# Two-block diffusion transformer on one core: the second block's mixer with hi and lo parts, two heads side by side, and both mLSTM directions in one tile

## The reference, cut to what matters

```python
def hybrid_mixer(h, w_in, gate_bias, g_q, g_k, g_mh, w_out):
    proj = (h @ w_in).astype(jnp.float32)
    mq, mk, mv, mo, mg, aq, ak, av = jnp.split(proj, idx, axis=-1)
    gates = mg.reshape(B, S, 4, M_HEADS).transpose(2, 0, 3, 1) + gate_bias[:, None, :, None]
    hm = bidirectional_mlstm(heads(mq, 4), heads(mk, 4) * (64 ** -0.5), heads(mv, 4),
                             gates[0], jax.nn.log_sigmoid(gates[1]), gates[2], jax.nn.log_sigmoid(gates[3]))
    hm = rms_norm(hm, g_mh) * jax.nn.sigmoid(mo)
    qa = partial_rope(rms_norm(heads(aq, 8), g_q), pos) * (64 ** -0.5)
    ka = partial_rope(rms_norm(heads(ak, 8), g_k), pos)
    ha = dilated_attention(qa, ka, heads(av, 8))
    return jnp.concatenate([hm, ha], axis=-1) @ w_out
```

## Time and profile before

| | us |
|---|---|
| median of 3 runs (lowest, highest) | 3451.45 (3450.44, 3454.13) |
| the profiled execution, its own time | 3450.88 |
| its span | 3449.1 |
| PE busy | 3188.1 (92%) |
| DVE busy | 1912.9 (55%) |
| ACT busy | 1013.9 (29%) |

### The profile page before, as it was taken

One profiled execution on the slowest core, in us unless ns is written; L12 is line 12 of the kernel. 1 busy time (PEld: TensorE's weight loads), 2 busy tenths in 40 slices (PEclk: granted clock), 3 DMA queues, 4 the chain that ended last, 5 costly groups with the idle time before them and its releaser, 6 DMA issues.

```text
span 3449.1 us, 36019 instructions
## 1 busy us (share of the span) xinstructions
PE 3188.1 (92%) x14535; PEld 2523.5 (73%) x14546; DVE 1912.9 (55%) x2700; ACT 1013.9 (29%) x1458; POOL 28.4 (1%) x31
## 2 busy tenths in 40 slices
PE   4999999898889999899969999799999989699998
PEld 3788888776677888788847888578877745377886
DVE  6876554645555554666565544566655534454444
ACT  2322122335442222322223222322223334232222
POOL 2000000000000000000000000000000000000000
PEclk6999999998999999999989999899999959699999
DMA  4443332110034433355512433145532200023221
GB/s 187 128 141 122 110 129 85 53 55 10 1 115 136 153 129 110 110 188 187 170 66 98 161 133 122 61 161 188 190 133 78 76 8 1 12 86 104 91 94 54
DMA packets 101889, 365.26 MB, mean 106 GB/s; under 512 B 11235, under 2 KB 12515, under 8 KB 101469
## 3 DMA queue, kind: packets, MB, share of 16 engines
q1 hardware_dynamic: 97644, 351.65, 30.7%
q10 hardware_dynamic: 2944, 6.29, 0.5%
q0 software_dynamic: 1136, 5.03, 0.4%
HBM read 360.83 MB, written 2.10 MB: 105 GB/s over the span
## 4 chain that ended last, share of the span: by engine, by line
PE 86%; DVE 9%; ACT 3%; issue 1%; DMA 1%; another core or an unknown queue 0%; ACTq 0%; POOL 0%; DVEq 0%; SPq 0%
PE ps L191 23%; PE ps L192 23%; PE ps L193 23%; PE ps L195 4%; PE ps L196 2%; DVE WL L183 1%; PE ps L2470 1%; DMA STG<-in_w_modt 1%; PE ps L2534 1%; DVE DUMP L304 1%; PE ps L2266 1%; PE ps L2269 1%; PE ps L507 1%; ACT WH L178 1%; DVE RAW L1301 1%
## 5 line engine op out<-in xcount | busy, mean ns | idle before, releaser
L191 PE MATMUL ps<-HH,WH 128*128 128x512 f32 x2464 | 980.3, 398 | 35.1 <-DVE HL L564 28.4
L192 PE MATMUL ps<-HL,WH 128*128 128x512 f32 x2464 | 968.9, 393 | 0.0
L193 PE MATMUL ps<-HH,WL 128*128 128x512 f32 x2464 | 968.6, 393 | 0.0
L178 ACT ACTIVATE WH<-RAW 128x1024 fp32r<-128x1024 f32 x456 | 456.7, 1047 | 569.0 <-PE ps L193 410.1
L183 DVE TENSOR_TENSOR WL<-RAW,WH 128x1024 fp32r<-128x1024 f32 x456 | 538.5, 1221 | 100.8 <-ACT WH L178 100.7
L191 PEld LDWEIGHTS ps<-HH,WH 128*128 128x128 f32 x2464 | 468.3, 190 | 144.3 <-issue 44.2
L192 PEld LDWEIGHTS ps<-HL,WH 128*128 128x128 f32 x2464 | 468.5, 190 | 100.3 <-issue 4.1
L193 PEld LDWEIGHTS ps<-HH,WL 128*128 128x128 f32 x2464 | 467.6, 190 | 100.9
L815 DVE SCALAR_TENSOR_TENSOR XT<-ps,DER,XT 128x512 f32<-128x512 f32 x512 | 342.9, 682 | 272.2 <-PE ps L193 257.7
L191 PE MATMUL ps<-GH,WH 128*128 128x512 f32 x1056 | 414.0, 392 | 19.1 <-DVE XT L815 14.3
L192 PE MATMUL ps<-GL,WH 128*128 128x512 f32 x1056 | 412.0, 390 | 0.0
(11 more groups left out here) (330 smaller groups left out, 2482.1 us busy)
## 6 DMA issues: line engine op xcount, KB each, us to landing
RAW<-in_w_modt SPq DMA_DIRECT2D x200, 512.0 KB, 4.6
RAW<-in_ffn_wi SPq DMA_DIRECT2D x176, 512.0 KB, 4.5
RAW<-in_ffn_wo SPq DMA_DIRECT2D x88, 512.0 KB, 4.7
RAW<-in_w_gu SPq DMA_DIRECT2D x88, 512.0 KB, 4.3
RAW<-in_w_in SPq DMA_DIRECT2D x44, 512.0 KB, 3.6
RAW<-in_w_down SPq DMA_DIRECT2D x44, 512.0 KB, 4.3
RAW<-in_w_out SPq DMA_DIRECT2D x16, 512.0 KB, 3.7
MU<-in_w_mod SPq DMA_DIRECT2D x8, 384.0 KB, 9.4
```

Of the source, the lines that this page charges most:

```text
L178: act.e.activation(u.hi, u.ld.view, ACT.Copy).then_inc(u.hi_done.sem, 1)
L191: pe.e.matmul(out, wh, x[0], start=first, stop=False)
L192: pe.e.matmul(out, wh, x[1], start=False, stop=False)
L193: m = pe.e.matmul(out, wl, x[0], start=False, stop=last)
```

## The change

- **Gates beside the projection.** `GT` becomes `G` with 36 partitions: the forward direction on partitions 0 to 3, the backward on 32 to 35. `MlGates`, `MlScan` and `MlTurnU` handle both directions together, and they are put into the list through `lag`, behind the first chunks of the projection. The log, the exponential and the scans stand in the mixer's first steps no more.
- **Hi and lo parts.** Queries and keys of both generators, the running maximum, the inverse denominators and the norm's factor are split by `HiLo` (hi on ACT, lo on DVE), and the matmuls on them become three (or two, where the other side is exact) in fp32r. The parts lie over `RAW` slots 2 to 5 and over the tensors that they replace.
- **Two heads side by side.** `DilScore`, `DilPV` and the new `DilQuot` issue the heads of a pair one behind the other, on array rows 0 to 63 and 64 to 127 (scores) or on array columns 0 to 63 and 64 to 127 (values). The values become the stationary operand, the output comes out already with features on partitions, and the division by the denominator is a product with a matrix that is spread by a matmul (`DilDen`, `DilQuot`) in place of a product and a transpose.
- **Sums of both directions together** (`MlSum`): two `A x V`, then two `A x 1`, the latter on 4 columns at array columns 0 and 32.
- **Order.** `dilated` goes first in `side_by_side`, has three pieces for each of 16 pairs, and every fourth round gives `mlstm` another piece. The split of the mLSTM half of `MIX` and of the first `w_out` tile is at the end of `mlstm`; the other half is split after the last `DilQuot`. The weight slots are 0 and 1 until the last score is done.

The core of the diff:

```diff
+class MlGates(Step):
+    def scalar(self, act):
+        m, t = self.m, self.t
+        act.wait_ge(*self.ready)
+        act.e.activation(m.EM, m.MG, ACT.Abs).then_inc(t[0].sem, 1)
+        act.wait_ge(*t[0])
+        act.e.activation(m.EM, m.EM, ACT.Exp, scale=-1.0).then_inc(t[1].sem, 1)
+        act.wait_ge(*t[1])
+        act.e.activation(m.EM, m.EM, ACT.Ln, bias=1.0).then_inc(t[2].sem, 1)
+class MlScan(Step):
+    def vector(self, dve):
+        m, t, rows = self.m, self.t, self.rows
+        dve.wait_ge(*m.gates)
+        dve.e.scalar_tensor_tensor(m.MG, m.MG, 0.0, m.EM, ALU.min, ALU.subtract).then_inc(t[0].sem, 1)
+        dve.wait_ge(*t[0])
+        dve.wait_ge(*m.ones)
+        for d in range(2):
+            dve.e.tensor_tensor_scan(rows(m.B, d), m.ONES[32 * d:32 * d + 4, :], rows(m.MG, d), 0.0,
+                                     ALU.mult, ALU.add).then_inc(t[1 + d].sem, 1)
+        dve.wait_ge(*t[2])
+        dve.e.tensor_tensor(m.U, m.U, m.B, ALU.subtract).then_inc(t[3].sem, 1)
+        dve.wait_ge(*t[3])
+        for d in range(2):
+            u = rows(m.U, d)
+            dve.e.tensor_tensor_scan(rows(m.MG, d), u, u, -BIG, ALU.max, ALU.max).then_inc(t[4 + d].sem, 1)
+        dve.wait_ge(*t[5])
+        dve.e.tensor_tensor(m.EM, m.B, m.MG, ALU.add).then_inc(t[6].sem, 1)
+    def scalar(self, act):
+        m = self.m
+        act.wait_ge(*self.t[6])
+        act.e.activation(m.EM, m.EM, ACT.Exp, scale=-1.0).then_inc(self.em.sem, 1)
...
 class MlBroadcast(Step):
-        pe.wait_ge(*m.scan[1].t[3])
-        pe.wait_ge(*m.landed)
+        pe.wait_ge(*m.sel)
+        pe.wait_ge(*self.split.done)
         for d in range(2):
+            r = slice(32 * d, 32 * d + 4)
             pe.wait_ge(*self.free[d])
-            pe.e.matmul(m.P.banks[1 + d], m.SEL[:, h, :], m.MG[:, d, :], start=True, stop=True).then_inc(self.spread[d].sem, 1)
+            pe.e.matmul(m.P.banks[1 + d], m.SEL[r, h, :], m.MGH[r, :], start=True, stop=False)
+            pe.e.matmul(m.P.banks[1 + d], m.SEL[r, h, :], m.MGL[r, :], start=False, stop=True).then_inc(self.spread[d].sem, 1)
...
-        p, par = h // 2, h % 2
-        r = slice(64 * par, 64 * par + 64)
+        p, r = h // 2, slice(64 * (h % 2), 64 * (h % 2) + 64)
+        js = slice(self.j * 128, self.j * 128 + 128)
+        pe.wait_ge(*m.qsplit.done)
+        pe.wait_ge(*m.ksplit.done)
         for t in self.qkfree:
             pe.wait_ge(*t)
-        pe.e.matmul(m.P.banks[0], m.K[r, p, self.j * 128:self.j * 128 + 128], m.Q[r, p, :],
-                    start=True, stop=True).then_inc(self.qk.sem, 1)
+        pe.e.matmul(m.P.banks[0], m.KH[r, p, js], m.QH[r, p, :], start=True, stop=False)
+        pe.e.matmul(m.P.banks[0], m.KH[r, p, js], m.QL[r, p, :], start=False, stop=False)
+        pe.e.matmul(m.P.banks[0], m.KL[r, p, js], m.QH[r, p, :], start=False, stop=True).then_inc(self.qk.sem, 1)
...
+class MlSum(Step):
+    def tensor(self, pe):
+        m, h, j = self.m, self.x.h, self.x.j
+        pe.wait_ge(*m.landed)
+        for d in range(2):
+            full = self.x.prod.full(d)
+            pe.wait_ge(*self.x.prod.done[d])
+            if j == 0:
+                pe.wait_ge(*self.free[d])
+            x = pe.e.matmul(m.P.banks[1 + d][:, full], m.V[:, j, h * 128:(h + 1) * 128], m.A[:, self.x.slot[d], full],
+                            start=j == 0, stop=True, skip_group_check=j > 0)
+        x.then_inc(self.summed.sem, 1)
+        for d in range(2):
+            full = self.x.prod.full(d)
+            x = pe.e.matmul(m.P.banks[3][32 * d:32 * d + 4, full], m.OH[:, 3 - h:7 - h], m.A[:, self.x.slot[d], full],
+                            start=h + j == 0, stop=True, skip_group_check=True)
+        x.then_inc(self.done.sem, 1)
...
 class DilScore(Step):
-        pe.e.matmul(b, w.Q[r, j, n * 128:(n + 1) * 128], w.K[r, j, :], start=True, stop=True)
...
+        def product(Q, K, first):
+            for par in range(2):
+                r = slice(64 * par, 64 * par + 64)
+                m = pe.e.matmul(w.P.banks[4 + par], Q[r, j, n * 128:(n + 1) * 128], K[r, j, :], start=first, stop=True,
+                                skip_group_check=not first)
+            return m
+
+        product(w.QH, w.KH, True)
         pe.wait_ge(*w.table)
+        for par in range(2):
+            pe.e.matmul(w.P.banks[4 + par], w.CB[:, 0:128], w.CB[:, 128 + o:128 + o + 512], start=False, stop=True,
+                        skip_group_check=True)
+        product(w.QH, w.KL, False)
+        product(w.QL, w.KH, False).then_inc(self.scored.sem, 1)
...
 class DilPV(Step):
-            m = pe.e.matmul(P.banks[7][:, hs * 64:hs * 64 + 64], w.PT[:, self.v % 3, i * 128:(i + 1) * 128],
-                            w.V[:, i, hs * 64:hs * 64 + 64], start=i == 0, stop=i == 3)
+            for par in range(2):
+                hs = 2 * j + par
+                m = pe.e.matmul(P.banks[7][64 * par:64 * par + 64, j * 128:(j + 1) * 128], w.V[:, i, hs * 64:hs * 64 + 64],
+                                w.PT[:, self.q % 2, par, i * 128:(i + 1) * 128], start=i == 0, stop=i == 3, skip_group_check=True)
...
+class DilDen(Step):
...
+            dve.e.tensor_tensor(w.D[:, 2 * par:2 * par + 2, :].rearrange("p r (h t) -> p r h t", t=128),
+                                w.P.ID.rearrange("p (a b t) -> p a b t", a=1, b=1).broadcast_to([128, 2, 2, 128]),
+                                w.DEN[:, s, par:8:2].rearrange("p (r h o) -> p r h o", h=2, o=1).broadcast_to([128, 2, 2, 128]),
+                                ALU.mult).then_inc(self.diag[par].sem, 1)
...
+class DilQuot(Step):
...
+            m = pe.e.matmul(P.banks[6][64 * par:64 * par + 64, :], P.ONE[:, 0:64], w.D[:, 2 * par:2 * par + 2, :],
+                            start=True, stop=True, skip_group_check=True)
...
+        x = w.MIX[:, 4:8, n * 128:(n + 1) * 128]
+        dve.wait_ge(*self.copied)
+        dve.wait_ge(*self.spread)
+        dve.e.tensor_tensor(x, x, w.P.banks[6].rearrange("p (c t) -> p c t", t=128), ALU.mult).then_inc(self.done.sem, 1)
...
+                def gates(ready):
+                    yield
+                    self.add(MlGates(m, ready))
+                    yield
+                    self.add(MlScan(m))
+                    yield
+                    yield
+                    self.add(MlTurnU(m, pr))
...
-            with ExitStack() as both:
-                self.add(Begin([self.group, self.roped, self.turned, self.evacd]))
-                m = Mlstm(self, both, MQt, MKt, MVt, MOt, GT, MIX)
-                w = Dilated(self, both, DQt, DKt, DVt, MIX)
-                self.side_by_side(self.mlstm(m), self.dilated(w, CF, cf), extra=5)
-                ready = [w.out[3].done, m.last]
-            return self.out_projection(mi, a["w_out_2"], MIX, ready, following)
-    def mlstm(self, m):
+            lent = [t for s in range(2, NRAW) for t in self.inslot[s].users]
+            self.add(Begin([self.group, self.roped, self.turned, self.evacd] + lent))
+            self.slots = [0, 1]
+            rounded = lambda n, shape, address: self.at(n, shape, F32R, address)
+            at = lambda n: self.address[n] if n in self.address else self.address[self.name(n)]
+            QH, KH = (rounded(n, [128, 4, T], at("RAW") + (2 + 2 * i) * 4096) for i, n in enumerate(("QH", "KH")))
+            QL, KL = rounded("QL", [128, 4, T], at("MIX") + 8192), rounded("KL", [128, 4, T], at("DKt"))
+            w = Dilated(self, outer, QH, QL, KH, KL, DVt, MIX, self.XT[:, 0:4, T:W])
+            m.tiles(outer, sb("MQH", [128, 2, T], F32R), rounded("MQL", [128, 2, T], at("MQt")),
+                    sb("MKH", [128, 2, T], F32R), rounded("MKL", [128, 2, T], at("MKt")))
+            mix = Mix(MIX, rounded("MH", [128, 8, T], at("MQt")), rounded("ML", [128, 8, T], at("MIX")))
+            self.side_by_side(self.dilated(w, CF, cf, DQt, DKt), self.mlstm(m, mix, a["w_out_2"]), extra=4)
+            self.slots = list(range(NRAW))
+            for s in range(2, NRAW):
+                self.inslot[s] = Lent([w.score[15].scored])
+            self.add(Begin([w.quot[3].done]))
+            self.add(MixSplit(self, mix, range(4, 8), [w.quot[3].done]))
+            self.out_products(mi, a["w_out_2"], mix, {}, following)
+        return [self.over]
+    def mlstm(self, m, mix, w_out):
         self.add(MlTables(m))
-        self.add(MlGates(m))
+        m.mgsplit = self.add(HiLo(self, m.MG, m.MGH[:, :], m.MGL[:, :], []))
+        m.qsplit = self.add(HiLo(self, m.Q[:, :, :], m.QH[:, :, :], m.QL[:, :, :], []))
...
+        for j in range(4):
+            w.qsplit[j] = self.add(HiLo(self, DQt[:, j, :], w.QH[:, j, :], w.QL[:, j, :], []))
+            w.ksplit[j] = self.add(HiLo(self, DKt[:, j, :], w.KH[:, j, :], w.KL[:, j, :], []))
+        last = len(w.pairs)
+        for q in range(last + 2):
+            if 1 <= q <= last:
+                self.add(DilCount(w, q - 1))
+            if q < last:
+                self.add(DilScore(w, q))
+                yield
```

(11 more changed lines are left out.)

483 lines of the change are left out of this document (237 added, 246 removed).

## The result

| | before | after |
|---|---|---|
| median of 4 runs, us (lowest, highest) | 3451.52 (3450.44, 3454.13) | 3399.76 (3399.12, 3401.05) |
| ratio, 95% interval | | 0.9849 (0.9832 to 0.9866) |
| span of the profiled execution, us | 3449.1 | 3397.7 |
| PE busy, us | 3188.1 | 3129.7 |

The account below looks back on a forecast made before the run. PE's work was taken to bound the projection and the mixer's first two stretches, a PE, DVE and ACT chain the tail. 3450.9 less 70 in the mixer plus 16 in the projection gave 3397 us, range 3368 to 3424.

Parts of the forecast that it names:

- The gates in the projection: Projection: gate work ahead of a weight split on ACT and a reciprocal on DVE delays PE, costing 16 us.
- The 2.5 us more for the clock: Projection: PE's pause lets its clock fall for a while, adding about 2.5 us to the 13.4 us delay.
- some 13 us: Projection: a PE gap of this length near 2622, given as a sign that would show the prediction right.
- The price of a pair: Dilated attention, two heads at full clock: scores 1.55, values and transposes 1.61, second head's transposes 0.43; 3.6 us.
- The price of a unit: mLSTM unit at full clock: score 0.8 and sums 2.3, so 3.1 us where it was 3.7.
- Phase 2: Mixer proper, fourth pair's score to last mLSTM sum: nine pairs, sixteen units, quotients, waits and clock; 92 us (80 to 105).
- the 5 us for a clock that rises late: Middle of the mixer proper: the clock rises about 10 us into this stretch, which costs 5 us.
- The rival with ACT and DVE in turn: Mixer's middle: ACT and DVE work in series, 112 us where 92 was forecast, total 3417; chance 0.14.
- Phase 1: Mixer proper, start to fourth pair's score, still at 1.2 GHz: 27 us (22 to 40), 5 of it waiting.
- Phase 3: Mixer's tail after the last mLSTM sum, with four dilated pairs in it: 63 us (50 to 72).
- the last two pairs, some 9.5 each on their chain: End of the tail: maximum, exponential, count, transposes and values of two dilated pairs, 19 us together.
- The output projection: After the mixer: it starts on the mLSTM half of MIX and a split weight tile, so nothing is added.

Follow-up runs that it names:

- the gap filled: Changed kernel plus six f32 matmuls on PE between the projection and the first dilated score, where PE stood still 5.2 us; 3399.42 us.
- the run with six pairs: Changed kernel with extra=2 for extra=4 until the last mLSTM sum, none after, so six dilated pairs stand in the tail, not four; 3411.79 us.
- the run with two: Kernel with gates in pieces and f32 scores (3385.99 us), with extra=0: two dilated pairs' scores stand behind the last mLSTM sum; 3379.97 us.

## Why the prediction was right, step by step

- **The gates in the projection** (forecast 16, measured 14.4). Each step came where it was put: `WH` 2617.39 for 2617.7, the end of `WL` 2619.7 for 2620.0, the reciprocal 2629.40 for 2629.6, the rotation 2633.60 for 2633.8, PE's next chunk 2636.18 for 2636.4. The 2.5 us more for the clock were 1.2 (14.4 less the 13.2 at 2636.18); behind the pause the first products do start further apart (2636.18, 2636.75, 2637.18, 2637.60, then 0.23 apart). The chain was followed instruction by instruction through the new order with durations from the trace, and so came out to 0.3 us. Only the sign was misnamed: the gap of "some 13 us" on PE is one of 7.42, since the 13.2 is how late PE is, 4.0 of it from the stall before.
- **The price of a pair** (forecast 1.55 for the scores, measured 1.54). The sum is right and its terms are not: the parts were put at 1.32 and take 1.00, the mask at 0.24 and takes 0.54. The 1.32 from the first block's window attention already had a small mask and its changes of mode in it (a product with `CB` of 128 columns at 838.88, which the rows leave out). So this is partly luck. That the heads overlap, as the rows had it, is shown by the run that puts them one behind the other.
- **The price of a unit** (forecast 3.1). The score is 0.78, the sums, 2.75 before, are 1.9 to 2.2 by the lengths of the two directions: 2.9 on average. I had taken half a us off the sums, and they lost 0.5 to 0.8.
- **Phase 2** (forecast 92, measured 82.1). Three terms were too large: the 5 us for a clock that rises late (it rose at 2805, with the phase), the waits (PE was idle 2.9 us for 4), and the units (16 x 0.2 = 3). The rival with ACT and DVE in turn is out: they are busy 42.4 and 42.6 us beneath PE's 79.2. The Trainium skill, "TensorEngine Tiling (Array Packing)", section "PSUM Bottleneck", has the reading of PSUM as a possible limit after a fourfold speedup by packing; with the twofold packing here it is not seen to act.
- **Phase 1** (forecast 27, measured 33.3). I summed PE's work at half clock. It is busy 22.0 us there, as summed; but I gave the waits 5 where they were 11.3, at the start for the splits of queries and keys, and then for the table load, the maximum and the exponential. With the gap filled the clock was 1.00 for about the first 9 us of the phase and nothing was won, so there the clock isn't the cause.
- **Phase 3** (forecast 63, measured 73.5). The mLSTM's part was right: 8.1 us to the first product (forecast 8.5), 25.0 for the heads (26), 10.0 for the norm (9.3). What failed is the end: "the last two pairs, some 9.5 each on their chain", 19. From the first `L2453` at 2930.64 to 2960.96 it is 30.3 us: 7.9 to the fifteenth pair's scores at 2938.49, for what stands in the queues ahead of them (half of the thirteenth pair's transposes, the twelfth's values, a quotient), then 9.7 and 12.8. The forecast had no term for the 7.9, and the last two pairs took 22.5 for 19. Pairs were taken as covered by the mLSTM's chain, on whose queues they stand in turn with it; the run with six pairs shows 8 us for each one more, the run with two shows 7.0 for each one less. The 73.5 also lies above the 72 that was given as this phase's bound.
- **The output projection** (forecast 0, measured 2.5 won): the clock at its start, 1.8 of it.

So the total came within 3 us, by errors of +6.3 and +10.5 against -9.9, -1.6 and -2.5. The mechanisms of the projection and of the middle were right; the sizes of the three phases were not, and in the tail the cover of the pairs wasn't there. The closeness of the total is in part luck. That the pitch of the middle is near the sum of PE's work, and the tail is not, was in rows 1 from the start (109.73 of 111.1 and 35.17 of 62.4).
